# A two-block transformer kernel: another order of the first units, scan tables spread over two units, scan lanes in cycles of four beats that run into the gate, and the powers of C on VectorE

## The reference, cut to what matters

```
h = rmsnorm(x, ln1_g);  q, k, v, u = split(h @ w_in)        # widths 1024, 256, 256, 1024
q, k = rmsnorm per head;  y_attn = sliding-window attention (window 128, sinks, bias from a table)
# S5 mixer on u, 64 groups of 16 channels, 64 complex states each:
lam  = exp(a * dt);  bb = f(lam, a) * b
s_t  = lam * s_(t-1) + bb @ u_t                               # along the 256 tokens
y    = gelu(Re(c @ s) + d * u);  y_ssm = y * sigmoid(y @ w_glu)
x = x + concat(rmsnorm(y_attn), rmsnorm(y_ssm)) @ w_out
# then the gated feed-forward of block 1, and a second block of two layers
```

## Time and profile before

| | us |
|---|---|
| median of three runs | 3356.32 |
| the profiled execution | 3355.99 |
| its span, first to last instruction | 3353.9 |
| PE busy | 3243.4 (97% of the span) |
| VectorE busy | 1866.0 (56%) |
| ScalarE busy | 1475.7 (44%) |
| GpSimd busy | 119.7 (4%) |
| mean granted TensorE clock | 0.987 of full speed |

### The profile page before, as it was taken

How to read it: one execution, slowest core, us unless ns; L and a number is a source line. 1 busy time by engine, 2 the same in 40 slices (tenths; PEclk the granted TensorE clock), 3 DMA queues, 4 the chain that set the end, 5 groups by cost and what they waited for, 6 DMA issues and landing times. The chain is left out here.

```text
span 3353.9 us, 38632 instructions
## 1 busy us (share of the span) xinstructions
PE 3243.4 (97%) x15842; PEld 2668.1 (80%) x15842; DVE 1866.0 (56%) x1958; ACT 1475.7 (44%) x1760; POOL 119.7 (4%) x99
## 2 busy tenths in 40 slices
PE   6988999999999999999999999999999999999998
PEld 5776788888888778878888888878787788888886
DVE  6555655555555544665555555565555655555555
ACT  5434444444444444444444444444444544444443
POOL 4230000000000000000000000000000000000000
PEclk9998999999999999999999999999999999999999
DMA  7333455555555555555555555545454555555554
GB/s 200 101 114 124 159 188 188 188 189 192 194 189 190 183 167 191 195 175 188 188 189 192 190 190 190 189 158 188 146 175 156 176 188 188 188 188 188 188 189 150
DMA packets 187548, 596.28 MB, mean 178 GB/s; under 512 B 12491, under 2 KB 19308, under 8 KB 186860
## 3 DMA queue, kind: packets, MB, share of 16 engines
q1 hardware_dynamic: 187372, 593.82, 54.6%
HBM read 588.54 MB, written 5.23 MB: 177 GB/s over the span
## 5 line engine op out<-in xcount | busy, mean ns | idle before, releaser
L1065 DVE TENSOR_TENSOR LO<-RAW,HI 128x1024 fp32r<-128x1024 f32 (+1 forms) x1104 | 1351.4, 1226 | 1156.0 <-ACT HI L578 1154.1
L578 ACT ACTIVATE HI<-RAW 128x1024 fp32r<-128x1024 f32 (+1 forms) x1104 | 1159.6, 1053 | 1370.9 <-PE PS L1886 1366.4
L1886 PE MATMUL PS<-HI,KPA 128*128 128x512 f32 x5376 | 1499.3, 395 | 18.4 <-issue 5.3
L1886 PEld LDWEIGHTS PS<-HI,KPA 128*128 128x128 f32 x5376 | 1008.8, 190 | 233.5 <-issue 16.6
L1886 PE MATMUL PS<-HI,KPB 128*128 128x512 f32 x3392 | 935.4, 392 | 4.0 <-DVE ACC L1561 3.4
L1886 PE MATMUL PS<-LO,KPA 128*128 128x512 f32 x2688 | 841.6, 394 | 9.8 <-DVE LO L1065 9.7
L1886 PEld LDWEIGHTS PS<-HI,KPB 128*128 128x128 f32 x3392 | 631.1, 188 | 133.0 <-issue 5.3
L1886 PEld LDWEIGHTS PS<-LO,KPA 128*128 128x128 f32 x2688 | 509.3, 190 | 121.8 <-DVE LO L1065 12.0
L1886 PE MATMUL PS<-LO,KPB 128*128 128x512 f32 x1696 | 524.3, 390 | 0.8 <-DVE KPB L1101 0.8
L1886 PEld LDWEIGHTS PS<-LO,KPB 128*128 128x128 f32 x1696 | 318.5, 188 | 68.8 <-issue 1.2
L605 ACT ACTIVATE KPB<-PS 128x512 fp32r<-128x512 f32 x98 | 58.6, 599 | 181.6 <-PE PS L1911 181.6
(11 more groups left out here) (255 smaller groups left out, 985.2 us busy)
## 6 DMA issues: line engine op xcount, KB each, us to landing
RAW<-in_w_up SPq DMA_DIRECT2D x128, 1024.0 KB, 5.1
RAW<-in_w_down SPq DMA_DIRECT2D x128, 1024.0 KB, 5.5
RAW<-in_w_qkv SPq DMA_DIRECT2D x48, 1024.0 KB, 5.1
RAW<-in_w_ff_gate SPq DMA_DIRECT2D x88, 512.0 KB, 3.9
RAW<-in_w_ff_up SPq DMA_DIRECT2D x88, 512.0 KB, 4.7
RAW<-in_w_ff_down SPq DMA_DIRECT2D x44, 1024.0 KB, 5.5
RAW<-in_w_in_ab SPq DMA_DIRECT2D x40, 1024.0 KB, 5.0
RAW<-in_w_in SPq DMA_DIRECT2D x16, 1024.0 KB, 5.9
```

Source lines behind the costliest of these rows:

```text
L578: e.activation(HI[:, s % NSPLIT, 0:w], RAW[:, d % NRAW, j, 0:w], ACT.Copy).then_inc(S("hi_made"), 1)
L1065: e.tensor_tensor(LO[:, h, 0:w], RAW[:, d % NRAW, j, 0:w], HI[:, h, 0:w].bitcast(F32), ALU.subtract).then_inc(S("lo_made"), 1)
L1886: ins = e.matmul(PS[:, b + j, 0:cw], l, r[:, h, 512 * j:512 * j + cw], start=(i == 0 and part == 0), stop=(last and part == 2))
```

## The change

`kv` becomes the first unit, before `u`, `q` and `glu`. `kv` feeds the chunks xT. B's zeroth powers go to a tile of their own, B0, and no longer to kv_sb. VectorE runs `angle()` (nine small operations) ahead of its first unit, spreads the operations on the eigenvalues and on B over the slots of `kv` and `u`, and takes the powers of C from GpSimd. The turns of B come in `u`, at one in a slot. The lanes have cycles of four beats, run in the slots of `q` and `glu`, and the products into the state of a chunk are issued ahead of those out of the one before. The norms of q run in `glu`; attention starts behind `glu` with six beats there. The chunks of `glu` are fed one step ahead. The bias rows are written behind the load of `u`'s steps 8 and 9.

```diff
-SCRATCH = 4096
+SCRATCH = 1024
+        u("kv", [(w_in, 1024, 512)], 0, 16, "a", "xT")
         u("u", [(w_in, 1536, 1024)], 0, 16, "a", "xT")
         u("q", [(w_in, 0, 1024)], 0, 16, "a", "xT")
-        u("kv", [(w_in, 1024, 512)], 0, 16, "a", "xT")
...
+    B0 = sb("B0", [128, 2, 512])
...
         for d in range(3, len(plan.dmas)):
             weights(d)
-            if d == dma_of("u", 12):
+            if d == dma_of("u", 8):
                 q.wait_ge(S("bias_rows_made"), 1)
                 e.dma_start(scratch[:, :, 0:383], bcast(WV[0:16, :], 1, 128)).then_inc(S("bias_written"), 16)
-            if d == dma_of("q", 0):
+            if d == dma_of("u", 4):
...
# ScalarE
+        def squares1():
+            for _ in range(5):
+                yield
+            sq = squares("ln1", x_loaded, JK1)
+            for _ in range(2):
+                next(sq)
+                yield
+            for _ in range(3):
+                yield
+            yield from sq
...
         def prep2():
-            q.wait_ge(S("trig_args"), 4)
+            q.wait_ge(S("squared"), NM["ln1"]["squared"] + 4)
+            spread_c(3, 3)
+            yield
...
+                yield
+                if b == 2:
+                    q.wait_ge(S("taps_done"), 2)
+                    spread_c(4, 0)
...
-        pr, sq1 = prep(), squares("ln1", x_loaded, JK1)
-        unit("u", feed("xT"), [pr, sq1], [pr, sq1], to_sb(lambda t: u_sb[:, t, :], "ln1"))
+        pr, sq1 = prep(), squares1()
+        unit("kv", feed("xT"), [pr, sq1], [sq1], to_sb(lambda t: kv_sb[:, t, :], "ln1"))
+        unit("u", None, [pr], [pr], to_sb(lambda t: u_sb[:, t, :], "ln1"))
         S0, S1, pr2 = ssm(0), ssm(1), prep2()
         unit("q", None, [pr2, S0, S1], (), to_sb(lambda t: q_sb[:, t, :], "ln1"))
-        qn = q_norm()
-        unit("kv", None, [S0, S1, qn], [qn], to_sb(lambda t: kv_sb[:, t, :], "ln1"))
-        drain(S0)
-        drain(S1)
+        qn, bk = q_norm(), late(back(), 5)
+        unit("glu", y_feed(), [S0, S1, qn, bk], [qn], ev_glu, ahead=1)
+        drain(bk)
         att = attn1()
-        unit("glu", y_feed(), [att, late(back(), 3), att], (), ev_glu, ahead=2)
-        for _ in range(2):
+        for _ in range(6):
             next(att)
# VectorE
+        def c_power(k):
+            a, b = c_of(k - 1)
+            c, d = c_of(k)
...
+            times(c, a, lre)
+            then(own(times(d, b, lre)))
+            q.wait_ge(S("c_spread"), k)
+            then(own(times(b, b, lim)))
+            yield
+            then(own(e.tensor_tensor(c, c, b, ALU.subtract)))
+            then(own(times(a, a, lim)))
+            e.tensor_tensor(d, d, a, ALU.add).then_inc(S("c_powers"), 1)
+            yield
...
+        angle()
         pr, ms1 = prep(), squares("ln1")
-        unit("u", feed("xT"), [pr, ms1], [pr, ms1])
+        unit("kv", feed("xT"), [pr, late(ms1, 8)], [ms1])
+        unit("u", None, [pr], [pr])
         S0, S1, pr2 = ssm(0), ssm(1), prep2()
         unit("q", None, [pr2, S0, S1])
         qn = q_norm()
-        unit("kv", None, [S0, S1, qn], [qn])
-        drain(S0)
-        drain(S1)
+        unit("glu", y_feed(), [S0, S1, qn], [qn], ahead=1)
         att = attn1()
-        unit("glu", y_feed(), [att, att], (), ahead=2)
...
-        for _ in range(2):
+        for _ in range(6):
             next(att)
# GpSimd: times, c_power and q_norm are gone
-        c_power(1)
         root("ln1")
-        for k in range(2, 5):
-            c_power(k)
         S0, S1 = ssm(0), ssm(1)
         unit("q", [S0, S1])
-        qn = q_norm()
-        unit("kv", [S0, S1, qn], [qn])
-        drain(S0)
-        drain(S1)
+        unit("glu", [S0, S1])
+        root("q")
         root("k")
# PE, the lane
+            for i in range(2):
+                into_state(0, i)
+                yield
+            for k in range(4):
+                yield
+                for i in range(2):
+                    if k < 3:
+                        into_state(k + 1, i)
+                    yield
+                out_of_state(k)
                 yield
...
-        unit("kv", None, [S0, S1])
-        drain(S0)
-        drain(S1)
+        bk = late(back(), 5)
+        unit("glu", None, [S0, S1, bk], ahead=1)
+        drain(bk)
         att = attn1()
-        unit("glu", None, [att, late(back(), 3), att])
-        for _ in range(2):
+        for _ in range(6):
             next(att)
```

More of the change, by code:

```diff
@@ L191, in make_banks @@
         turn = 0
[L192 removed]
+        pairs = [0, 2]
         for u in self.units:
[L194 removed]
+            if u.name == "qkv1.0":
                 pairs, turn = [0, 2], 0
@@ L634, in to_sb, with expand, turned_b @@
             return evac
+        def expand(n):
+            s, part = PARTS[n]
+            if n % 2 == 0:
+                q.wait_ge(S("b_powers"), min(n // 2 + 1, 3))
+            if n >= 2:
+                q.wait_ge(S("xb_turned"), n - 1)
+            src = B0[:, part, :] if s == 0 else BB[:, (0, 2, 0)[s - 1] + part, :]
+            for g in range(2):
+                ins = e.activation(XB[:, part, :, 16 * g:16 * g + 16], src.rearrange("p (j c) -> p j c", c=16),
+                                   ACT.Copy, scale=par("group", g, 1))
+            ins.then_inc(S("xb_made"), 1)
+        def turned_b(n):
+            s, part = PARTS[n]
+            q.wait_ge(S("xb_turned"), n + 1)
+            if s == 0:
+                q.wait_ge(S("trig_args"), 4)
+            for hf in range(2):
+                e.activation(BLT[:, s, part, 4 * hf:4 * hf + 4, :].rearrange("p a b -> p (a b)"), PS[:, 4 + hf, :],
+                             ACT.Copy).then_inc(S("bl_made"), 1)
         def prep():
@@ L650, in prep @@
             yield
-            spread_c(1, 1)
+            yield
+            yield
             for n in range(9):
                 if n < 8:
[L654 to L663, removed]
-                if n:
-                    s, part = PARTS[n - 1]
-                    q.wait_ge(S("xb_turned"), n)
-                    if s == 0:
-                        q.wait_ge(S("trig_args"), 4)
[L669 to L674, removed]
-                yield
+                    expand(n)
+                if n:
+                    turned_b(n - 1)
+                if n == 3:
+                    yield
+                    yield
+                yield
+            spread_c(1, 1)
+            yield
+            yield
+            q.wait_ge(S("bias_written"), 16)
+            spread_c(2, 2)
+            yield
[5 more added lines that the diff above has]
+                next(sq)
+                yield
+            for _ in range(3):
+                yield
+            yield from sq
         def spread_c(power, slot):
@@ L1123, in times, with angle @@
             return e.tensor_tensor(small3(out), small3(in0), bcast(lam, 2, 16), ALU.mult)
[L1125 to L1128, removed]
+        v1, v2, v3, v4, v5, v6 = (sp[f"v{i}"] for i in range(1, 7))
+        ang, mag, qf, fre, fim, q4 = (sp[n] for n in ("ang", "mag", "qf", "fre", "fim", "q4"))
+        def angle():
             c1 = 6.28125
@@ L1223, in ssm @@
         def ssm(p):
-            for _ in range(5 if p else 2):
+            for _ in range(6 if p else 4):
                 yield
@@ L1927, in x_loaded, with turn_b @@
             q.wait_ge(S(f"x_loaded{c // 4}"), 16)
+        def turn_b(n):
+            s, part = PARTS[n]
+            q.wait_ge(S("ident_loaded"), 16)
+            q.wait_ge(S("xb_made"), n + 1)
+            q.wait_ge(S("bias_rows_made"), 1)
+            q.wait_ge(S("bl_made"), 2 * n)
+            for k in range(8):
+                ins = e.transpose(PS[:, 4 + k // 4, (k % 4) * 128:(k % 4) * 128 + 128],
+                                  XB[:, part, 4 * k:4 * k + 4, :].rearrange("p j c -> p (j c)"), ID[:, :])
+            ins.then_inc(S("xb_turned"), 1)
         def prep():
-            for _ in range(4):
+            for _ in range(12):
                 yield
@@ L1976, in ssm, with u4, into_state @@
         def ssm(p):
-            if p == 0:
-                yield from u_turn()
-            else:
-                for _ in range(5):
-                    yield
             ba = 4 + 2 * p
             state = lane_view(LANE[p][0])
-            for k in range(4):
-                kc = 2 * k + p
-                u4 = uT[:, kc, :].rearrange("p (c s) -> p c s", s=4)
-                y4 = PS[:, ba, 0:256].rearrange("p (c s) -> p c s", s=4)
+            def u4(k):
+                return uT[:, 2 * k + p, :].rearrange("p (c s) -> p c s", s=4)
+            def into_state(k, i):
                 q.wait_ge(S("uT_made"), 4)
@@ L2011, in ssm @@
                         rows = slice(32 * r, 32 * r + 32)
-                        e.matmul(y4[rows, :, tap:4], KT[rows, kc, tap, :], u4[rows, :, 0:4 - tap], start=(tap == 0), stop=False)
+                        e.matmul(y4[rows, :, tap:4], KT[rows, kc, tap, :], u[rows, :, 0:4 - tap], start=(tap == 0), stop=False)
                 q.wait_ge(S("c_spread"), 5)
```

(16 more changed lines are left out.)

179 lines of the change are left out of this document (78 added, 101 removed).

## The result

The changed kernel takes **3361.53 us** (median of 20 runs, 3360.11 to 3363.26), the kernel before 3355.74 in the same comparison (20 runs): ratio 1.0017, 95% interval 1.0010 to 1.0024. It is a little slower; the forecast was 3349. The profiled execution took 3362.97 us with a span of 3360.9.

The account below looks back on a forecast made before the run. PE, nearly always busy, loses time at the start, in u, at kv's end and around attention. Terms 44.6 + 72.5 + 96.6 + 36.2 + 17 + 92.5 put wa0 at 359.4 against 366.1, 6.7 us less: 3349 us, range 3335 to 3366.

Parts of the forecast that it names:

- `ws0`, `ws1` and the rest of attention: From ws0's first matmul to wa0: 76.1 us before, plus 13.4 for groups 0 and 1, plus 3.0 tail, 92.5 us.
- The start and `kv`: Up to u's first matmul: angle() delays PE's first LO part 2.3 us, VectorE sets kv's end; 44.6 us, bounds 41 to 49.
- `u`: Stage u: PE stalls 14.3 us behind the bias write after step 8; 72.5 us in all, bounds 58 and 78.
- does not stop PE: Rival in u: the bias write causes no stall, VectorE bounds u at about 59 us, 13.5 less; 3335 us, chance 0.10.
- Powers of C: In u: 18 operations moved to VectorE at 0.69 us each, 12.4 us of its time, charged 0.5 us.
- `q` and the gate: Stages q and glu: q full with steps and scan blocks, 96.6 us; glu with the scan's rest, 36.2 us.
- Gap: Between glu and ws0: chain of root, normalisations, sums of k, second root, products, turns and scores; 17 us, bounds 13 and 24.
- attention is exposed: Rival, glu's last matmul to wa0: longer preparation, more waits and slow clock, slow tail add 17 us; 3366 us, chance 0.20.

Follow-up runs that it names:

- the pieces: Changed kernel with the bias-row write split into four pieces of 32 copies, behind the loads of u's steps 4, 6, 8 and 10: 3345.31 us.
- late attention: Kernel before with attention taken out of the gate stage, starting behind it with six beats there: 3371.21 us, ratio 1.0049.
- the placing: One of two attention beats put between a step's halves on PE in ws0, ws1: changed kernel 3348.65 us; kernel before with attention behind the gate 3360.79.
- the norms' other work: Changed kernel with the norms of k and q (squares, sums, roots, products) moved to the gate stage's first beats, k first: 3355.10 us, ratio 0.9998.

## Why the prediction was wrong

Five of the six terms held within 2 us. The step that failed is **"`ws0`, `ws1` and the rest of attention"**, 92.5 us forecast, 103.75 measured: 11.25 of the 12.7 us by which `wa0` was missed.

- *The start and `kv`*: right, 44.71; `angle()` cost 2.4 us at PE's first LO part, forecast 2.3.
- *`u`*: the stall by the bias write was 14.66 us, forecast 14.3, and by its parts too: issued at 50.86 (51.4), PE on its way at 92.35 (92.4). With the pieces the stall is gone. The Trainium skill (DMA: Bandwidth & Descriptors, Specifications) would have the 1532 B rows at line rate; 3064 KB in 35.4 us, about 89 GB/s, is again far from the 407 GB/s of the earlier trace rows. The write as a whole costs more than the rival "does not stop PE" had it: with the pieces `u` takes 55.4 us, 17.5 less, where the rival had 59, 13.5 less.
- *Powers of C*: 0.69 us an operation as taken. They were priced only as a load on VectorE; put back on GpSimd they cost 9 us, because the copy that frees PE's banks waits behind them.
- *`q` and the gate*: 132.8 us forecast, 132.9 measured. That the sum is so close is in part luck: `q` was 1.8 us shorter and the gate 1.9 longer.
- *Gap*: 17.85 for 17, by the chain that was named.
- *Attention*: I took the cost of group 0 from a row of the gate stage, 12.3 us with a wait of 3.09, and 3 us for the tail, the three beats behind `ws1`. PE's busy time in the stretch grew by 15.8 us (84.5 against 68.7) and its idle time by 11.9 (19.3 against 7.4); the forecast had 16.4 for both together. Here it is sorted by group from PE's timelines, each group with its waits, against the same work before. Of the 12.3 us for group 0, 1.8 at the slow clock have a row of their own, and the 0.9 of scores in the gap are off:

| added to the 76.1 us of before | forecast | measured |
|---|---|---|
| group 0, without the scores in the gap | 9.6 | 12.6 |
| group 1 | 2.0 | 5.9 |
| group 2 | 0 | 0.0 |
| group 3, with the tail | 3.0 | 6.0 |
| main matmuls (lower clock) | 1.8 | 2.6 |
| the rest | 0 | 0.5 |
| sum | 16.4 | 27.6 |

The bad phase, in which turn and output share a slot, is not what was missed: group 0 had it in the earlier trace rows, and group 2 had it before as well. It waited 2.53 us then and 2.52 now:

```profile
321.90 0.43 PE L2087 MATMUL PS<-kv_sb,PT 128*128 128x64 f32 x2 [2.53 <-ACT PT L783]
```
```profile
337.39 0.69 PE L2124 MATMUL PS<-kv_sb,PT 128*128 128x64 f32 x2 [2.52 <-ACT PT L805]
```

Missed were three things that are queued at the new place and were not at the old. *Group 0*, 3.0 us over its price: 4.28 us of wait at 286.03, for a copy of ScalarE that now has a square of YS, `ws0`'s input, (L820) ahead of it besides exponentials, a feed and an HI; and 1.4 us of waits for the exponentials (0.2 before). ScalarE between the turns at 281.20 and the output:

```profile
283.51 1.05 ACT L580 ACTIVATE HI<-RAW 128x1024 fp32r<-128x1024 f32 x1
284.45 1.06 ACT L820 ACTIVATE SQT<-YS 128x1024 f32<-128x1024 f32 x1
...
285.49 0.48 ACT L805 ACTIVATE PT<-PS 128x384 f32<-128x384 f32 x1
```

*Group 1*, 3.9 us over: its second turn falls on the end of `ws0` and waits 3.20 us at 316.14, where it had waited 0.41. VectorE has the evacuation of `ws0` ahead of the result that it waits for:

```profile
313.13 2.47 DVE L1436 SCALAR_TENSOR_TENSOR XR<-PS,ST,XR 128x1024 f32<-128x1024 f32 x2
315.52 0.48 DVE L1408 TENSOR_TENSOR q_sb<-PS,ST 128x128 f32<-128x128 f32 x2
```

*The tail*, 3.0 us over: its three beats took 10.2 us (359.85 to 370.03), where the same beats took 4.2 in the slots of `ws1`. From the last matmul of `ws1` to `wa0` it is 13.4 us, before 1.4, with 3.9 of waits (1.38 of them for a copy behind the evacuation of `ws1`) and turns at the lower level (1.83 us for six, 0.82 elsewhere). The long waits were followed by matmuls at that level, 1.2 GHz: the two at 316.46 took 1.20 us, 0.61 to 0.73 elsewhere. The window's granted clock is 0.86 where the earlier trace rows has 0.94.

That late attention is the cause is shown by its run on the kernel before. That it is these queues is read from the timelines; no run takes the square or an evacuation away.

The rival "attention is exposed" is what happened: 121.6 us from the gate's end to `wa0`, forecast 109.5 by the sum and 126.5 by the rival (its 17 us more), total 3366 by the rival against 3361.5. It was right on the place and in the main on the size, but its parts were others: it had two more groups pay 3.09 us and the slow clock, and the new waits of group 1 and of the tail stand at the ends of `ws0` and `ws1`. My reason against it, that groups 1 and 3 keep their phase, held and did not help: in that phase an output and the next turn share a slot, and the turn of group 1 waited 3.20 us for the output's result.

The Trainium skill (Perfetto Trace Analysis, Matmul Optimizations) advises matmuls back to back in batches, because the engine scales power with utilization. The runs agree with the reason, not with a long batch as such: shorter batches with less idle time between them gave a granted clock of 0.92 for 0.86 in one order, 0.87 for 0.86 in the other, and both were faster.

Open: how much of the placing's 10 to 13 us is clock, and what made the executions differ ahead of `ws0`, by 1.9 us in one order and 3.9 in the other.

## What to carry over

A block moved behind its old place must be priced by its chain at the new place: write down, engine by engine, what is queued ahead of each copy that a matmul waits for, the evacuation at a unit's end above all, and put half a step of products between a turn and its output. A tail with nothing beside it costs its waits and the lower clock on top of its instructions: 10.2 us here for beats that had taken 4.2. And a long write in a queue of loads belongs in pieces between them.

## What was not expected of the hardware

- The write of 3064 KB took 33.9 us in the kernel before and 35.4 in the changed one, though it started elsewhere. In four pieces each took 15.6 us from issue to landing (median) with loads between them, and the stall was still gone.
- Two roots in a row on GpSimd (8 and 32 columns) took 8.03 us in the gate's stage, against 1.64 + 5.44 apart. With the norms' other work the stage took 39.6 us instead of 38.1.
- The window of the gate has a granted clock of 1.00, the gap behind it, with PE busy for 10.7 of 18 us, one of 0.64.
